# Mixture-of-experts blocks of 130 to 150 rows, sized by the expert's rank, in a one-layer streaming encoder step

## The reference

```python
pg = softmax(x @ w_rg + b_rg); pg_top, g_idx = top_k(pg, 1)          # 1 of 4 groups
le = (x @ w_re + b_re).reshape(B, L, 4, 4)[group g_idx]
pv, pi = top_k(softmax(le), 2); pv = pv / sum(pv)                    # 2 of its 4 experts
gates = pg_top * one_hot(g_idx) * inner                              # 16 experts, two not zero
for e in range(16):
    hid = silu(x @ w_gate[e]) * (x @ w_up[e])                        # 1024 -> 512
    y = y + gates[..., e:e + 1] * (hid @ w_down[e])                  # 512 -> 1024
```

## Time and profile before

| | us |
|---|---|
| median of 3 runs | 1008.7 (1007.33 to 1008.98) |
| the profiled execution, its own time | 1008.3 |
| its span from the first to the last instruction | 1006.7 |
| mixer and router | 0 to 545 |
| table, first gather, first turn | 545 to 561 |
| the 16 blocks | 561 to 959 |
| tail | 959 to 1007 |

### The profile page before, as it was taken

How to read it: one execution, slowest core, us unless ns; L and a number is a source line. 1 busy time by engine, 2 the same in 40 slices (tenths; PEclk the granted TensorE clock), 3 DMA queues, 4 the chain that set the end, 5 groups by cost and what they waited for, 6 DMA issues and landing times. The chain is left out here.

```text
span 1006.7 us, 16592 instructions
## 1 busy us (share of the span) xinstructions
PE 905.0 (90%) x6409; PEld 788.3 (78%) x6409; DVE 433.8 (43%) x1183; ACT 161.4 (16%) x456; POOL 211.0 (21%) x307
## 2 busy tenths in 40 slices
PE   6979999999999999999982699999999999999900
PEld 3964878769596886959651699999999999999900
DVE  2242464636436463643667322222233333322278
ACT  2121222121312122121221001100100000000023
POOL 2040030300303020030302322222222222221251
PEclk9989999999999999999996799999999999999955
DMA  9970706052100101010071998888888888888866
GB/s 333 295 244 1 240 2 184 27 184 58 63 1 16 49 1 43 1 43 1 1 293 48 72 363 315 307 301 301 301 303 305 311 308 312 313 312 311 312 224 235
DMA packets 91903, 184.52 MB, mean 183 GB/s; under 512 B 12933, under 2 KB 59589, under 8 KB 83666
## 3 DMA queue, kind: packets, MB, share of 16 engines
q1 hardware_dynamic: 72930, 154.86, 44.2%
q0 software_dynamic: 7328, 19.22, 6.5%
q10 hardware_dynamic: 11600, 9.84, 3.0%
HBM read 142.56 MB, written 41.31 MB: 183 GB/s over the span
## 5 line engine op out<-in xcount | busy, mean ns | idle before, releaser
L1253 PE MATMUL bank<-wout,win 128*128 128x150 f32 x2048 | 266.1, 291 | 18.2 <-DVE wout L1143 16.0
L1253 PEld LDWEIGHTS bank<-wout,win 128*128 128x128 f32 x2048 | 264.0, 190 | 18.7 <-issue 18.7
L1253 PE MATMUL bank<-hT,win 128*128 128x128 f32 (+1 forms) x1536 | 182.4, 279 | 0.0
L1253 PEld LDWEIGHTS bank<-hT,win 128*128 128x128 f32 x1536 | 178.5, 192 | 1.5 <-issue 1.2
L1253 PE MATMUL bank<-win 128*128 128x150 f32 x1024 | 133.6, 290 | 0.0
L1253 PEld LDWEIGHTS bank<-win 128*128 128x128 f32 x1024 | 132.0, 189 | 0.0
L1253 PE MATMUL bank<-win,hT 128*128 128x260 f32 (+3 forms) x512 | 121.7, 416 | 4.9 <-DVE hT L797 2.8
L1182 DVE TENSOR_TENSOR win<-bank,win 128x150 f32<-128x150 f32 x64 | 20.0, 315 | 244.7 <-ACT win L744 244.7
L1253 PE MATMUL bank<-wout,mixT 128*128 128x512 f32 (+1 forms) x384 | 117.2, 487 | 1.8 <-ACT mixT L682 1.7
L1253 PEld LDWEIGHTS bank<-win,hT 128*128 128x128 f32 (+1 forms) x512 | 77.0, 173 | 45.4 <-issue 32.7
L1253 PEld LDWEIGHTS bank<-wout,mixT 128*128 128x128 f32 (+1 forms) x384 | 51.0, 163 | 58.1 <-issue 55.4
(11 more groups left out here) (268 smaller groups left out, 760.5 us busy)
## 6 DMA issues: line engine op xcount, KB each, us to landing
win<-in_w_gate SPq DMA_DIRECT2D x32, 1024.0 KB, 5.0
win<-in_w_up SPq DMA_DIRECT2D x32, 1024.0 KB, 7.1
win<-in_w_down SPq DMA_DIRECT2D x32, 1024.0 KB, 7.9
ye_d<-zeros SPq DMA_DIRECT2D x4, 4352.0 KB, 18.5
ye_d<-wout ACTq DMA_DIRECT2D x64, 150.0 KB
win<-in_w_in SPq DMA_DIRECT2D x4, 2048.0 KB, 19.6
xbuf<-in_x_prompt SPq DMA_DIRECT2D x8, 512.0 KB, 3.8
wout<-in_w_out SPq DMA_DIRECT2D x1, 4096.0 KB, 15.5
```

The source lines that it names most:

```text
L1253: return nc.tensor.matmul(out, lhsT, rhs, start=first, stop=last)
```

## The change

Experts are ranked by row count, and the blocks have fixed sizes by rank. Expert 0 always stands first with 150 rows (its rows can be gathered before the counts are known). Behind it come six blocks of 130 rows, three of 135, two of 140 and four of 150. Rows that don't fit an expert's block go to further blocks of 150 behind these. The counts above fit their blocks exactly as ranked (130: 107, 119, 124, 125, 125, 126; 135: 127, 129, 133; 140: 133, 140; 150: 140, 144, 146, 148), so there are 16 blocks and no further one. In all they have 2215 rows, where 16 x 150 was 2400.

Since the sizes are constants, the loops of TensorE, ScalarE and VectorE each become a series of loops, one for each size. TensorE's start at fixed positions of the fetch blocks of its code, and TensorE reads the number of blocks only ahead of the last loop. Gather and weight loads stay one loop, and a gather still fetches 5 x 32 rows.

The core of the diff:

```diff
-    NB = NE + (2 * TOK - NE) // BLOCK
+    SLOTS = ((30, 1), (26, 6), (27, 3), (28, 2), (30, 2))
+    NS = sum(n for _, n in SLOTS)
+    SIZES = [NP * r for r, n in SLOTS for _ in range(n)] + [BLOCK] * (NE - NS)
+    YBASE = [sum(SIZES[:p]) for p in range(NE + 1)]
+    NB = 2 * NE + 1
-    YROWS = -(-NB * BLOCK // P) * P
+    YROWS = -(-(YBASE[NE] + (NB - NE) * BLOCK) // P) * P
...
@@ ScalarE: one loop for each size @@
+            def expert(j, r, base):
+                n = NP * r
...
-                    a.activation(sgl[:, f % 2, :], B[GB[f]][:, 0:BLOCK], ACT.Silu).then_inc(silu_ready, 1)
+                    a.activation(sgl[:, f % 2, 0:n], B[GB[f]][:, 0:n], ACT.Silu).then_inc(silu_ready, 1)
...
+            for r, count in SLOTS:
+                with act.Fori(j0, j0 + count) as j:
+                    expert(j, r, j * (NP * r) + (YBASE[j0 - 1] - NP * r * j0))
+                j0 += count
+            with act.Fori(NS + 1, nblocks + 1) as j:
+                expert(j, RP, j * BLOCK + (YBASE[NS] - BLOCK * (NS + 1)))
...
@@ VectorE: the table, ahead of first_turn @@
+            link(v.scalar_tensor_tensor(out=key, in0=cnt[:, :], scalar=float(NE), in1=iof[:, 0:NE], op0=ALU.mult, op1=ALU.add))
+            link(v.memset(key[:, 0:1], -1.0))
+            link(v.tensor_tensor(cube[:, 0], across(key), wide(key, [P, NE, NE]), ALU.is_lt))
+            link(v.tensor_reduce(out=pos, in_=cube[:, 0], axis=AX.X, op=ALU.add))
+            link(v.tensor_tensor(cube[:, 0], across(iof[:, 0:NE]), wide(pos, [P, NE, NE]), ALU.is_equal))
+            link(v.tensor_tensor(cube[:, 1], cube[:, 0], across(szv[:, 0, :]), ALU.mult))
+            link(v.tensor_reduce(out=size, in_=cube[:, 1], axis=AX.X, op=ALU.add))
...
+            link(v.tensor_tensor(over, cnt[:, :], size, ALU.subtract))
...
@@ VectorE: behind first_turn @@
+            products(1, SLOTS[0][0])
+            turn(1)
+            link(v.tensor_tensor(thr, ecap[:, :], size, ALU.add))
+            link(v.tensor_tensor(row1, base, ecap[:, :], ALU.subtract))
...
             for n in range(2):
-                link(v.tensor_tensor(picks, oh[:, :, n, :], rowof[:, :].unsqueeze(1).broadcast_to([P, NT, NE]), ALU.mult))
-                link(v.tensor_reduce(out=rt[:, NT * n:NT * n + NT], in_=picks, axis=AX.X, op=ALU.add))
+                for c, x in enumerate((thr, row1, row2)):
+                    link(v.tensor_tensor(picks, oh[:, :, n, :], x.unsqueeze(1).broadcast_to([P, NT, NE]), ALU.mult))
+                    link(v.tensor_reduce(out=rt[:, NT * c:NT * c + NT], in_=picks, axis=AX.X, op=ALU.add))
...
+            results(1, SLOTS[0][0])
+            nblocks = dve.value_load(tabi[0:1, 2 * NJ:2 * NJ + 1], min_val=NE, max_val=NB)
+            for r, count in SLOTS[1:]:
+                with dve.Fori(j0, j0 + count) as j:
+                    products(j, r)
+                    turn(j)
+                    results(j, r)
+                j0 += count
...
@@ TensorE @@
-            after(pe, "table_ready", 1)
-            nblocks = pe.value_load(tabi[0:1, 2 * (NB + 1):2 * (NB + 1) + 1], min_val=0, max_val=NB)
-            with pe.Fori(1, nblocks + 1) as j:
+            def expert(j, r):
+                N = NP * r
...
-                                last = mm(B[GB[f]][:, n * BLOCK:(n + 1) * BLOCK].rearrange("p (a i) -> p a i", a=NP),
-                                          w[:, k, f * P:(f + 1) * P], xgT[:, k, :, 0:RP], n == 0 and k == 0,
+                                last = mm(B[GB[f]][:, n * N:(n + 1) * N].rearrange("p (a i) -> p a i", a=NP),
+                                          w[:, k, f * P:(f + 1) * P], xgT[:, k, :, 0:r], n == 0 and k == 0,
...
+            PE_ONLY, HEAD = [mybir.EngineType.PE], {mybir.EngineType.PE: 0}
+            for r, count in SLOTS:
+                with nc.Fori(j0, j0 + count, engines=PE_ONLY, head_slot=HEAD) as j:
+                    expert(j, r)
+                j0 += count
+            after(pe, "table_ready", 1)
+            nblocks = pe.value_load(tabi[0:1, 2 * (NB + 1):2 * (NB + 1) + 1], min_val=NE, max_val=NB)
+            with nc.Fori(NS + 1, nblocks + 1, engines=PE_ONLY, head_slot=HEAD) as j:
+                expert(j, RP)
```

138 lines of the change are left out of this document (83 added, 55 removed).

## The result

| | kernel before | changed kernel |
|---|---|---|
| median of the runs | 1008.84 us (1007.33 to 1009.3) | 994.15 us (992.76 to 995.83) |
| profiled execution | 1008.3 us, span 1006.7 | 995.25 us, span 993.6 |
| first block starts | 560.98 | 563.69 |
| first block | 29.16 us | 28.81 us |
| blocks 2 to 15 | 343.10 us | 327.05 us |

The ratio is 0.986, with a 95% interval of 0.984 to 0.988. The change is faster by 1.4%, but the time lies just above the range of 977 to 993, and half of the forecast gain is missing. The two spans (the time from the first to the last instruction of the profiled execution) differ by 13.1 us. Blocks 2 to 15 gave 16.1 and the first block 0.35; the later start took 2.7 and the end 0.6.

The account below looks back on a forecast made before the run. The prediction took the sixteen blocks to be bound by TensorE's matmuls: 1008.3 - 28.5 (narrower matmuls) + 0.6 (yslot chain) = 980.4, with 0.4 for the median 980.8 us; range 977 to 993.

Parts of the forecast that it names:

- 1. Narrower matmuls: TensorE's 192 matmuls a block, at 130, 135 or 140 columns instead of 150: gain 28.5 us, ends 26.2 and 29.9.
- 2. Who is late next: Other engines and DMA beside a shortened block of 21.5 us: all hidden or fitting, nothing charged.
- the turn: VectorE's pass over the next block's gathered rows, before that block starts: hidden, with 2.4 us left.
- the stores: ScalarE's four result stores and table reload, ahead of the next block's first Silu: hidden by 1.5 us or more.
- the weights: Weight halves for the next block: landing in 7.0 us, with 7 us to spare in the short block.
- 3. The table: VectorE's longer table ahead of the first block: ends at 554.8, covered by the wait for gathered rows; cost 0.
- 4. The yslot chain: VectorE's 9.0 us chain, now behind the first block's turn, delays block 2's first Silu to 604.1; 0.6 us charged.
- 5. Loops in series: Series of loops, branch and register at five more places, larger zero fills, twelve constants: 0 charged.
- Each new loop pays a first pass: Rival: each of five new loops has the first pass's 2.24 us of issue gaps, 11.2 us; 992.0 us, chance 0.08.
- A ceiling of 310 GB/s: Rival: DMA can't exceed 310 GB/s, so a 130-row block needs 24.3 us; about 1007 us, chance 0.05.
- Code fetched on each turn: Rival: TensorE refetches its loop's code in 15 further blocks, 2.24 us each, 33.6 us; 1014.4 us, chance 0.03.
- a further block: Rival: a token routed otherwise overfills an expert's block, adding a block of 150, 24.5 us; 1005.3 us, chance 0.02.

Follow-up runs that it names:

- e3: The changed kernel with GpSimd making only the first of the five gathers in each block behind the first; 982.05 us.
- f2: The changed kernel with TensorE waiting for the table again, and three gathers instead of five for each later block; 980.62 us.
- g1: The changed kernel with TensorE waiting for the table again, and four gathers instead of five for each later block; 982.02 us.
- h2: The changed kernel with TensorE waiting for the table, no load of later token numbers (same rows gathered each time) and a sixth gather into an unused tile; 1011.1 us.
- f5: The changed kernel with TensorE waiting for the table, and the five gathers started only halfway through the block's gate and up products; 993.81 us.
- e2: The changed kernel with TensorE's five loops of fixed size (blocks 1 to 14) written out as straight code; 992.82 us.

## Why the prediction was wrong, step by step

**1. Narrower matmuls: right.** Without the holes blocks 2 to 15 take 314.16 us, 28.9 less than before, where the step said 28.5. The price at 130 columns was 111.7 ns (112.0 taken), at 135, 140 and 150 as forecast, and the cut of the operand in five pieces costs nothing. The weight load's 106.7 ns, by the Trainium skill (TensorE: Matmul & The Clock Gate, LDWEIGHTS), is not the distance that is seen: the traces have 111.7 at 128 columns and at 130.

**2. Who is late next: this step failed.** It went through the turn, the stores, the weights and the bytes, and each of these four was in time. What runs beside TensorE and delivers in time was put at nothing. That holds above all for GpSimd, which the earlier trace rows show busy for 90 of 374 us and whose gathers the step never priced, without a reason. But beside them TensorE lost 0.7 to 1.5 us in each of ten blocks, and 0.6 in two more together: 12.9 us. Between the spans, where the sum has 1006.7 - 28.5 + 0.6 = 978.8 and 993.6 was measured, 14.8 us are missing: 12.9 of holes, 2.7 of the later start and 0.6 at the end, less 0.35 in the first block, 0.4 in step 1 and the 0.6 of step 4. The one sign in the trace of before was the first block's two gaps put down to "issue". I gave them a cause by their place (the first pass through the loop) and priced them only there. They also stood 1.8 and 5.3 us behind the last of five gathers, and go with their number: none with one gather (e3), 0.5 us with three (f2), 1.1 with four (g1), 0.8 to 3.1 with five, 3.4 with six (h2), split rows and f5 left aside. Whether they have the same cause as the holes, which take ScalarE's stores too, is not shown.

**3. The table: right.** It ended at 554.41 + 0.14 = 554.55, where 554.8 was worked out, and the rows landed later than it. But PE did not start near 561. What was early was TensorE: freed from the table, it fetched code beside the scatter, and that took 1.3 to 2.1 of the 2.7 us. The step looked at the wait that was moved on VectorE's side and not at what TensorE does sooner without it.

**4. The yslot chain: right in its working, wrong in its end.** It took 9.0 us, from 589.08 to 598.1, and the first Silu came at 604.51 for 604.1. It cost nothing, since block 2 itself started at 592.50 instead of 590.1. ScalarE doesn't load its table there any more, so the cover is 1.3 us wider than I took it.

**5. Loops in series: right.** Each costs two packets in its first block and none on its turns, and e2 without loops gains at most 2.0 us in blocks 2 to 15. The end of the program is 0.6 us longer; I did not look into that. **The rivals.** "Each new loop pays a first pass" would have given 992.0, near the time, but for a wrong reason: the holes are in every block of a loop, and remain without loops. A ceiling of 310 GB/s is refuted by 331. Code fetched on each turn is refuted by eleven packets; a further block did not appear. That the range all but reached the time is luck: it was the price of this rival, and not of the holes, that drew its upper end. All four rivals together missed the mechanism.

**What stays open.** Shown for the blocks behind the first is that a row of five gathers, with ScalarE's stores beside it, makes TensorE stand still at 130 to 140 columns, that four gathers don't, that five of a sixteenth of the bytes do, that a pause of 1.9 us in the row or three quarters of the stores left out takes the holes away or nearly so, and that loops and branches are not needed. That what stops is the supply of TensorE's instructions is my reading of "issue" and of the 43 to 48 matmuls that still run; no row shows the instructions themselves. Why five gathers of the same rows spare TensorE and six don't, what makes the gaps of the first block, and what the engines' instructions share with these gathers, no run here tells.

## What to carry to other kernels

When the bounding engine gets faster, don't only ask who must deliver to it: ask also what runs beside it that it does not wait for. A gap put down to "issue" is a price without a known owner, and the cheapest test of an owner is to take away part of the suspect (here one gather instead of five), not to reason from the gap's place. And a wait that is removed lets its engine run ahead: look at what it will then fetch or start, and beside whom.

## What the runs showed of the hardware that I had not expected

- With GpSimd's five gathers of 128 rows, 1.25 us apart, and four stores of ScalarE beside them TensorE stands still for 0.7 to 1.5 us in a block of 130 to 140 columns, without a wait that the profile shows; a sixth gather makes it 2.5 to 2.7 us at 130 columns, four make nothing. Five gathers of the same rows each time make nothing either, but the six were of the same rows, too.
- Beside a fetch of 16 KB of instructions (1.69 us) two packets of 4 and 32 bytes came 1.6 us late, in each of the three kernels with such a fetch 1.3 to 1.6, and with them the chain to TensorE's first block by 1.3 to 2.1 us.
- Matmuls of 128 and 130 columns are 111.7 ns apart; from 135 columns on it is 0.84 ns a column.
- A VectorE operation of 0.31 us took 2.75 beside two GpSimd operations on 512 columns (1.07 us each).
